# Two-block transformer kernel on one core: expert weight slots that give each partition two neighbouring rows

## The chip, the cores and the metric

The kernel runs on one core of a Trainium2 chip. The metric is the device time of one execution in microseconds (us), lower is better; a run's time is the median over several executions. Every time below is in us unless it is marked ns.

## The reference, cut to what matters

The program computes two transformer blocks on 512 rows of 1024 floats, all in float32. The first block has two layers. Each layer has a mixer (two attentions, a short convolution and gates) and then an expert layer in which each of 16 experts chooses its rows:

```
logits = einsum('bnd,de->ben', h, w_router); aff = softmax(logits, axis=1)
gate, idx = top_k(aff, cap)            # cap = 2 n / 16: 64 rows of x, 32 of the context
xs = h[idx]                            # gather: 16 experts x cap rows x 1024
a = einsum('becd,edf->becf', xs, w_g)  # w_g, w_u, w_d: 16 x 1024 x 1024 each, per layer
u = einsum('becd,edf->becf', xs, w_u)
y = einsum('becf,efd->becd', silu(a) * u, w_d)
out = zeros.at[idx].add(y * gate)
```

Layer 0 does this for x (64 rows per expert) and for the context (32 rows per expert) with the same weights; layer 1 for x alone. The expert weights are 3 x 16 x 4 MB = 201 MB in each layer, and every byte of them is read once per layer. The second block has two more attentions and a dense feed-forward layer; it has no experts.

## The kernel before, in words

Five engines run five programs written out by hand. They meet by semaphores, and nothing reorders them: the order on an engine is the order of its program. SyncE (SP) issues nearly all the transfers. TensorE (PE) does the products, the gathers (a product with a matrix of zeros and ones) and the turns (transposes by a product with the identity).

**Where the expert weights go.** An expert weight is cut into pieces of 256 rows x 1024 columns, 1 MB each. A piece goes by one transfer into one slot: 128 partitions x 2048 floats, read as `p (k n)` with k = 2. `expert_loads(l)` makes the list of the 192 pieces of a layer: for each expert four pieces of the gate and four of the up matrix by turns (`inner`, 8 pieces), and after each even expert from the third on the 8 pieces of the down matrices of a pair (`down`). Before the change, partition p of a slot holds rows p and p + 128 of the piece, each a run of 4096 bytes in memory. `sp_experts` (L2640 issues) walks this list: for each piece it waits until the former piece of that slot has been multiplied, and issues the transfer. Layer 1 has 12 slots for its first 12 pieces and 7 that go round after that.

**Who reads them.** `pe_inner` multiplies the gathered rows of expert x with the 8 pieces of its gate and up matrices: for each piece it waits for the arrival, then for k in (0, 1) it takes the 128 contraction rows `kk = 2 * k2 + k`. L1925 and L1928 are these products in layer 0 and L1920 in layer 1. `pe_outer` does the same with the down matrices of a pair (L1959 and L1964 in layer 0, L1955 in layer 1), and frees two slots at a time. `pe_back` (L1850, L1854) puts the results back into the rows of x.

**Who decides which rows of the contraction a tile holds.** The gathers write the gathered rows with the contraction (the 1024 features) over the partitions: tile k takes 128 feature columns of the normalised rows `H2h`, `H2l` (high and low part) as the stationary operand, and the choice matrix `SX` or `SC` as the moving one. L1546 is the gather of the context (layer 0, 32 matmuls), L1572 in `pe_gather` is the gather of x (128 matmuls in layer 0; 64 in layer 1 ahead of the experts, and 192 more, in 24 steps of 8, between the products of experts 1 to 9: `late_steps`, `pe_late`). The turns of `pe_flip` (L1900) do the same for the hidden rows ahead of the down product: tile j takes 128 columns of `hw`, as the stationary operand, against the identity (6 turns per expert in layer 0, 4 in layer 1).

Two operations elsewhere in the program are of use for comparison. L2276, in the second block, turns tiles of `XT` whose stationary operand takes every fourth column, 16 bytes apart. The table `k_rope` is loaded once, 1 MB with 2048 floats (8192 bytes) in one run per partition.

Names used below: e0 and e1 are the expert stages of layers 0 and 1. A row `ps<-sx,h2h` is a matmul whose moving operand is `sx` and whose stationary one is `h2h`; its LDWEIGHTS row (PEld) loads the stationary one.

Of the kernel before, what the change touches and what calls it, by code (L numbers as in the profile page):

```python
# [236 lines left out]
def build(nc, I, cst, cmask, crope, at, out):  # L237
    ctx = ExitStack()
    with ctx:
# [43 lines left out]
        def signals(*names):  # L283
            made = [Signal(sem(n)) for n in names]
            SIG.extend(made)
            return made
# [9 lines left out]
            "d_wg", "d_xo", "r_dve", "e_hb", "e_ht", "e_st", "d_lz", "d_ff", "d_an", "d_out")  # L296
        l_rc, l_na, l_ma, l_h2, l_an = signals("l_rc", "l_na", "l_ma", "l_h2", "l_an")

        class Mem:
            pass  # L300

# [38 lines left out]
        for l in (0, 1):  # L340
# [3 lines left out]
            n = (2, 4)[l]  # L344
# [11 lines left out]
        ident = K("ident")  # L356
# [31 lines left out]
        SX, SXf = (sx[:, :].bitcast(t).rearrange("p (t e c) -> p t e c", t=4, e=16) for t in (F32R, F32))  # L388
        SC, SCf = (sc[:, :].bitcast(t).rearrange("p (t g r e c) -> p t g r e c", t=2, g=8, r=2, e=2) for t in (F32R, F32))
# [63 lines left out]
        def expert_loads(l):  # L453
            found = []

            def add(name, src, *freed):
                srcs = [(lambda b: b.rearrange("p (k n) -> p k n", k=2), src.rearrange("(k p) n -> p k n", p=128))]
                found.append((name, ES[l].add(srcs, SLOT, "plain", freed)))

            def inner(e):  # L460
                for k2 in range(4):
                    for w, name in enumerate(("w_e_gate", "w_e_up")):
                        add(("in", e, k2, w), I[name][l][e][256 * k2:256 * k2 + 256, :], e_in, f"e{l}", e, k2, w)

            def down(p):
                for f2 in range(4):
                    for x in (0, 1):
                        add(("dn", p, f2, x), I["w_e_down"][l][2 * p + x][256 * f2:256 * f2 + 256, :], e_dn, f"e{l}", p, f2)

            for e in range(NE):  # L470
                inner(e)
                if e % 2 == 0 and e:
                    down(e // 2 - 1)
            down(NE // 2 - 1)
            return found
# [998 lines left out]
        def pe_choice(e, l):  # L1474
# [7 lines left out]
            ps, when = bank.take((st, "lgp"), r_act.at(st, "lgp"))  # L1482
# [4 lines left out]
            for k in range(KD):  # L1487
                e.wait_ge(*r_act.at(st, "h", k))
                for a, b in segs(T):
                    i = e.matmul(ps[32 * (k % 4):32 * (k % 4) + 32, a:b], wr[:, 128 * l + 16 * k:128 * l + 16 * k + 32], HT[:, k, a:b],  # L1490
                                 start=k < 4, stop=k > 3, skip_group_check=True)
            i.then_inc(*p_rt.up(st, "lgp"))
            mods(*range(80, 88))
            ps, when = bank.take((st, "lg"), r_dve.at(st, "af"))
# [3 lines left out]
            for c in range(ntc):  # L1498
                i = e.matmul(ps[:, 16 * c:16 * c + 16], L_[1][:, 128 * c:128 * c + 128], K("fold"), start=c == 0, stop=True, skip_group_check=True)
# [3 lines left out]
            ps, when = bank.take((st, "E"), r_dve.at(st, "E"))  # L1503
# [3 lines left out]
            for c in range(ntc):  # L1507
                i = e.transpose(ps[0:16, 128 * c:128 * c + 128], affT[:, c, :], ident)
            i.then_inc(*p_rt.up(st, "E"))
            for c in range(ntc):  # L1510
                ps, when = bank.take((st, "h2", c), r_act.at(st, "h2", c))
                for w in when:
                    e.wait_ge(*w)
                for k in range(KD):
                    i = e.transpose(ps[:, k * 128:(k + 1) * 128], HT[:, k, c * 128:(c + 1) * 128], ident)
# [4 lines left out]
            ps, when = bank.take((st, "mk"), r_dve.at(st, "m"))  # L1520
# [3 lines left out]
            for c in range(ntc):  # L1524
                i = e.transpose(ps[:, 16 * c:16 * c + 16], L_[3][0:16, c * 128:(c + 1) * 128], K("ident")[0:16, 0:16])
            i.then_inc(*p_rt.up(st, "mk"))
            ps, when = bank.take((st, "cum"), r_dve.at(st, "pos"))
# [4 lines left out]
            for a, b, cap, c0, c1 in sides:  # L1532
                for j in range(c0, c1 - 1):
                    i = e.matmul(ps[:, 16 * j + 16:16 * c1], ones[:, :], mskT[:, j:j + 1, :].broadcast_to([128, c1 - 1 - j, 16]), start=False,
                                 stop=j == c1 - 2, skip_group_check=True)
            i.then_inc(*p_rt.up(st, "cum"))
            if l == 0:
                e.wait_ge(*r_dve.at(st, "sc", 1))
                e.wait_ge(*l_h2.at(st, ntc - 1))
                for k in range(KD):  # L1540
                    ps, when = bank.take((st, "xc", k), r_act.at(st, "xc", k))
                    for w in when:
                        e.wait_ge(*w)
                    for c in (0, 1):
                        for p, h2 in enumerate((m.H2h, m.H2l)):
                            i = e.matmul(ps[:, 0:512], h2[:, 4 + c, k * 128:(k + 1) * 128], SC[:, c, :, 0].rearrange("p g e c -> p g (e c)"),  # L1546
                                         start=c == 0 and p == 0, stop=c == 1 and p == 1)
                    i.then_inc(*p_rt.up(st, "xc", k))
            e.wait_ge(*l_h2.at(st, ntc - 1))
# [4 lines left out]
            for tiles in jobs:  # L1554
                taken = []
                for k, part in tiles:
                    ps, when = bank.take((st, "xs", k, part), gathered(l, k, part))
                    taken.append(ps)
                    for w in when:
                        e.wait_ge(*w)  # L1560
                for c in (1, 2, 3, 0):
                    e.wait_ge(*r_dve.at(st, "sx", c))
                    for ps, (k, part) in zip(taken, tiles):
                        pe_gather(e, l, ps, k, part, c)

        def gathered(l, k, part):
            return (r_dve if (k % 2 if l else part) else r_act).at(f"e{l}", "xs", k, part)

        def pe_gather(e, l, ps, k, part, c):
            m, n = ME[l], 4 if l else 8  # L1570
            for p, h2 in enumerate((m.H2h, m.H2l)):
                i = e.matmul(ps[:, 0:64 * n], h2[:, c, k * 128:(k + 1) * 128], SX[:, c, n * part:n * part + n, :].rearrange("p e c -> p (e c)"),  # L1572
                             start=c == 1 and p == 0, stop=c == 0 and p == 1)
            if c == 0:
                i.then_inc(*p_rt.up(f"e{l}", "xs", k, part))
# [7 lines left out]
        def pe_late(e, k, part):  # L1583

            e.wait_ge(*c_lz.at("e1", last_round(1) - 1))
            if k:
                e.wait_ge(*r_act.at("e1", "xs", k - 1, part))
            elif part > 1:
                e.wait_ge(*r_act.at("e1", "xs", KD - 1, part - 1))
            for c in (1, 2, 3, 0):  # L1590
                pe_gather(e, 1, late_tile, k, part, c)
# [134 lines left out]
        P0, P1, PC, P3 = bank.tiles  # L1726
# [158 lines left out]
        def pe_flip(e, l, x):  # L1885
            st = f"e{l}"
            if x == 0:
                e.wait_ge(*c_lz.at(st, last_round(l) - 1))
            if x:
                e.wait_ge(*e_ht.at(st, x - 1))  # L1890
            if l == 0:
                if x:
                    e.wait_ge(*e_si.at(st, x - 1, "hc"))
                p = (x - 1) // 2 - 1
                if p >= 1 and p % 2 and x % 2:
                    e.wait_ge(*d_xo.at(st, p, KD - 1))
            e.wait_ge(*e_hb.at(st, x))
            hw = HW1[x % 3] if l else HW0[x % 2]
            for j in range(4 if l else 6):
                i = e.transpose(P3[:, 128 * j:128 * j + 128], hw[:, 128 * j:128 * j + 128], ident)  # L1900
            i.then_inc(*e_tr.up(st, x))

        def pe_inner(e, l, x):
# [64 lines left out]
        def pe_experts(e, l):  # L1968
            st = f"e{l}"
            for tile, freed in bank.queue:  # L1970
                for w in freed:
                    e.wait_ge(*w)
            for x in range(NE):
                pe_inner(e, l, x)
                if l and x:
                    pe_flip(e, l, x - 1)
                p = x // 2 - 1
                if x % 2 == 0 and x:
                    pe_outer(e, l, p)
                if x % 2 and p >= 0 and batch(l, p):  # L1980
                    pe_back(e, l, p)
            pe_flip(e, l, NE - 1)
            pe_outer(e, l, MANY - 1)
            pe_back(e, l, MANY - 1)
            read = (d_xo.at(st, MANY - 1, KD - 1),)
            normed = (n_ln.at(f"n{l + 1}"),)
            bank.start((normed, read, read, read) if l else (read, read, normed, read))
# [589 lines left out]
        def pe_program(e):  # L2577
            pe_start(e)
            for l in (0, 1):
                pe_proj(e, l)  # L2580
                projected(e, l)
                pe_attention(e, AT[l])
                attended(e, l)
                pe_merge(e, l)
                pe_choice(e, l)
                pe_experts(e, l)
            pe_second(e)
# [143 lines left out]
```

## Time and profile before

| | |
|---|---|
| time, median of 3 runs | 3599.14 us (3598.61 to 3600.02) |
| span of the profiled execution | 3596.7 us |
| PE busy | 3375.6 us, 94% of the span |
| PE weight loads (PEld) | 2272.8 us, 63% |
| DVE, ACT, POOL busy | 35%, 28%, 5% |
| moved by DMA | 601.35 MB, of which 403 MB are expert pieces (384 of 1 MB) |

The span goes from the first to the last instruction of one execution. No other time of that execution is given; the timed runs are 2.4 us longer at their median, which is what lies around the span. A busy share is an average over stages with different limits; the busy time of PE also counts matmuls whose ends are modelled.

### The profile page before, as it was taken

Reading aid. Unit: us, or ns where it says so; the run is one execution under the profiler, and the core shown is the slowest. Engines: PE = TensorE matmul, PEld = TensorE weight load, DVE = VectorE, ACT = ScalarE, POOL = GpSimd, SP = SyncE. Lnnn points to the kernel's source line nnn. Section 1 sums busy time; section 2 is a strip of 40 time slices with the busy share of each in tenths; the row PEclk is TensorE's granted clock in tenths of the full one; section 3 lists DMA queues with packets and bytes.
Section 4 is the critical chain, followed back from the end, with each engine's and each line's share of the span. In section 5 each row is a group of like instructions: output and inputs, shape, how many; then the busy total and the mean of one; then the engine's idle time right before and its main releaser. Section 6 shows DMA issues by size and latency. Waiting matters only on the chain.

```text
span 3596.7 us, 48683 instructions
## 1 busy us (share of the span) xinstructions
PE 3375.6 (94%) x21614; PEld 2272.8 (63%) x21618; DVE 1241.8 (35%) x1745; ACT 1023.8 (28%) x1641; POOL 197.5 (5%) x118
## 2 busy tenths in 40 slices
PE   7999999999899999989999998898879999989998
PEld 5787667887544443467768874333227766868887
DVE  3235642223421111144563343111124434353333
ACT  3523541213310000036353232000012344243323
POOL 0100000211100000001000221000001010020000
PEclk9999999999899999999999998999999999999999
DMA  7440014222499889822102327999992121323332
GB/s 227 132 139 24 1 51 123 61 65 88 172 372 400 345 340 398 333 65 81 37 1 77 94 82 290 409 408 409 409 336 76 37 57 30 97 62 94 99 98 67
DMA packets 360129, 601.35 MB, mean 167 GB/s; under 512 B 48786, under 2 KB 242672, under 8 KB 359792
## 3 DMA queue, kind: packets, MB, share of 16 engines
q1 hardware_dynamic: 357024, 596.62, 46.8%
q8 instruction: 171, 2.80, 0.3%
q10 hardware_dynamic: 2896, 1.61, 0.2%
q14 instruction: 38, 0.31, 0.0%
HBM read 596.09 MB, written 2.10 MB: 166 GB/s over the span
## 4 chain that ended last, share of the span: by engine, by line
PE 85%; DMA 7%; DVE 5%; ACT 2%; issue 1%; ACTq 0%; POOL 0%; DVEq 0%; SPq 0%
PE ps L581 32%; PE ps L1925 6%; PE ps L2303 5%; PE ps L1075 4%; PE ps L1920 4%; PE ps L633 3%; PE ps L1164 3%; PE ps L1928 3%; PE ps L1959 3%; PE ps L1125 3%; PE ps L1339 3%; DMA ring<-in_w_e_down 3%; DMA ring<-in_w_e_up 2%; PE ps L602 2%; PE ps L1955 2%; PE ps L1850 2%
## 5 line engine op out<-in xcount | busy, mean ns | idle before, releaser
L581 PE MATMUL ps<-xh,wh 128*128 128x512 f32 x1912 | 647.2, 377 | 20.0 <-DVE xl L2142 9.8
L581 PE MATMUL ps<-xh,wl 128*128 128x512 f32 x1912 | 631.6, 368 | 0.0
L581 PE MATMUL ps<-xl,wh 128*128 128x512 f32 x1912 | 630.1, 368 | 0.0
L554 DVE TENSOR_TENSOR wl<-ring,wh 128x1024 fp32r<-128x1024 f32 (+1 forms) x259 | 333.9, 1289 | 441.0 <-ACT wh L545 439.4
L581 PEld LDWEIGHTS ps<-xh,wh 128*128 128x128 f32 x1912 | 330.4, 189 | 105.9 <-issue 33.3
L545 ACT ACTIVATE wh<-ring 128x1024 fp32r<-128x1024 f32 (+1 forms) x259 | 271.9, 1050 | 424.1 <-PE ps L581 163.2
L581 PEld LDWEIGHTS ps<-xl,wh 128*128 128x128 f32 x1912 | 329.8, 189 | 63.5 <-issue 4.5
L581 PEld LDWEIGHTS ps<-xh,wl 128*128 128x128 f32 x1912 | 329.5, 189 | 61.4
L1925 PE MATMUL ps<-ring,arena 128*32 128x512 f32 x2048 | 267.3, 594 | 1.0 <-DVE arena L1707 1.0
L1920 PE MATMUL ps<-ring,arena 128*64 128x512 f32 x984 | 227.0, 599 | 17.4 <-DMA ring<-in_w_e_up 8.7
L1920 PEld LDWEIGHTS ps<-ring,arena 128*64 128x64 f32 x984 | 66.6, 137 | 155.3 <-issue 102.7
L1928 PEld LDWEIGHTS ps<-ring,arena 128*32 128x32 f32 x2048 | 66.8, 110 | 152.9 <-issue 152.9
L1086 DVE TENSOR_REDUCE sm<-ps 128x2 f32<-128x1536 f32 (+3 forms) x96 | 142.3, 1482 | 50.4 <-PE ps L1075 50.2
L1928 PE MATMUL ps<-ring,arena 128*32 128x256 f32 x2048 | 157.5, 379 | 0.0
L1075 PE MATMUL ps<-arena 64*128 64x256 f32 (+3 forms) x800 | 152.1, 455 | 2.6 <-DVE arena L1035 1.8
L1125 PE MATMUL ps<-consts,tmp 128*128 128x128 f32 x832 | 127.1, 285 | 20.3 <-DVE arena L1181 12.0
L1104 ACT ACTIVATE tmp<-ps,sm 128x768 f32<-128x768 f32 (+3 forms) x176 | 132.5, 761 | 46.2 <-DVE sm L1089 38.8
L1955 PE MATMUL ps<-ring,arena 128*64 128x512 f32 x512 | 119.3, 618 | 26.6 <-DMA ring<-in_w_e_down 18.9
L2080 DVE SCALAR_TENSOR_TENSOR y<-ps,gate,y 128x1024 fp32r<-128x1024 f32 x16 | 20.5, 1284 | 306.8 <-ACT y L2015 306.8
L1125 PEld LDWEIGHTS ps<-consts,tmp 128*128 128x128 f32 x832 | 88.5, 141 | 58.9 <-issue 21.9
L1959 PE MATMUL ps<-ring,hbuf 128*32 128x512 f32 x1024 | 121.8, 592 | 0.8 <-DVE hbuf L2072 0.8
L1463 POOL TENSOR_TENSOR arena<-arena,tmp 128x768 f32<-128x768 f32 (+1 forms) x32 | 65.8, 2058 | 991.3 <-DVE tmp L1421 991.3
(278 smaller groups left out, 4329.8 us busy)
## 6 DMA issues: line engine op xcount, KB each, us to landing
ring<-in_w_e_gate SPq DMA_DIRECT2D x128, 1024.0 KB, 9.4
ring<-in_w_e_down SPq DMA_DIRECT2D x128, 1024.0 KB, 8.7
ring<-in_w_e_up SPq DMA_DIRECT2D x123, 1024.0 KB, 9.3
ring<-in_w_in SPq DMA_DIRECT2D x116, 512.0 KB, 3.9
ring<-in_w_ada SPq DMA_DIRECT2D x96, 512.0 KB, 4.7
ring<-in_w_ff SPq DMA_DIRECT2D x64, 512.0 KB, 3.9
ring<-in_w_out SPq DMA_DIRECT2D x24, 512.0 KB, 3.6
ring<-in_w_in SPq DMA_DIRECT2D x40, 256.0 KB, 3.9
```

The lines of the kernel that those rows point to most:

```text
L545: e.activation(m.WH[:, o:o + many], halves.aps[s][:, 0:many], ACT.Copy).then_inc(*hi.up(X.key, q))
L554: e.tensor_tensor(m.WL[:, o:o + many], halves.aps[s][:, 0:many], m.WH[:, o:o + many].bitcast(F32), ALU.subtract).then_inc(*lo.up(X.key, q))
L581: i = e.matmul(ps[0:M, a:b], w[:, k, 0:M], h[:, k, a:b], start=k == 0 and p == 0, stop=k == 7 and p == 2)
L1075: x = e.matmul(ps[:, col:col + k.shape[-1]], q, k, start=first, stop=last, skip_group_check=True)
L1086: e.tensor_reduce(mx, A.units(i, A.scores(i)), AX, ALU.max).then_inc(*a_rm.up(A.stage, i))
L1125: x = e.transpose(ps[:, 128 * c:128 * c + 128], src[:, u, 128 * b:128 * b + 128], ident)
L1920: i = e.matmul(pa[64 * h:64 * h + 64, 512 * w:512 * w + 512], rows_of(1, kk, x, 0, 64), W[:, k, 512 * h:512 * h + 512], start=kk == 0, sto ...
L1925: e.matmul(pa[64 * h + g:64 * h + g + 32, 512 * w:512 * w + 512], rows_of(0, kk, x, g, g + 32), W[:, k, 512 * h:512 * h + 512], start=kk = ...
L1928: i = e.matmul(pb[32 * q:32 * q + 32, 256 * w:256 * w + 256], rows_of(0, kk, x, 64, 96), W[:, k, 256 * q:256 * q + 256], start=kk == 0 and ...
L1955: i = e.matmul(ps[64 * x:64 * x + 64, 512 * h:512 * h + 512], HT2[p % 2][:, x, k % 4, k // 4, :], w, start=k == 0, stop=k == 7)
L1959: e.matmul(ps[64 * x + g:64 * x + g + 32, 512 * h:512 * h + 512], HX[:, k, 64 * x + g:64 * x + g + 32], w, start=k == 0, stop=k == 7, skip ...
L2303: i = e.matmul(ps[:, n:n + 512], ff_part(h, f)[c], w[:, 0, n:n + 512], start=f == 0 and p == 0, stop=f == 31 and p == 2, skip_group_check= ...
```

## The change

It touches four lines and adds a helper. The transfer of an expert piece now gives partition p rows 2p and 2p + 1 of the piece, which lie side by side in memory: one run of 8192 bytes instead of two of 4096. The slot is as large as before, its address and the number of transfers too. The products still read the slot by k = 0 and 1, so that k now stands for the even and the odd rows of the piece. To match, the tile that is multiplied with k must hold every second feature: `woven(k)` takes, out of the 256 columns of a piece, every second one, beginning at k % 2. It stands in the gathers of the context and of x and in the turns, each time as the stationary operand, whose columns are then 8 bytes apart instead of 4. Instructions, their order, their waits and their sizes are the same on PE, DVE, ACT and POOL; on SP the 384 transfers of expert pieces read 128x2048 instead of 128x2x1024.

```diff
@@ in build
+        def woven(k, o=0):
+
+            a = o + 256 * (k // 2) + k % 2
+            return slice(a, a + 255, 2)
@@ in expert_loads
             def add(name, src, *freed):
-                srcs = [(lambda b: b.rearrange("p (k n) -> p k n", k=2), src.rearrange("(k p) n -> p k n", p=128))]
+                srcs = [(lambda b: b, src.rearrange("(p k) n -> p (k n)", k=2))]
@@ in pe_choice (the context's gather, L1546)
-                            i = e.matmul(ps[:, 0:512], h2[:, 4 + c, k * 128:(k + 1) * 128], SC[:, c, :, 0].rearrange("p g e c -> p g (e c)"),
+                            i = e.matmul(ps[:, 0:512], h2[:, 4 + c, woven(k)], SC[:, c, :, 0].rearrange("p g e c -> p g (e c)"),
@@ in pe_gather (L1572)
-                i = e.matmul(ps[:, 0:64 * n], h2[:, c, k * 128:(k + 1) * 128], SX[:, c, n * part:n * part + n, :].rearrange("p e c -> p (e c)"),
+                i = e.matmul(ps[:, 0:64 * n], h2[:, c, woven(k)], SX[:, c, n * part:n * part + n, :].rearrange("p e c -> p (e c)"),
@@ in pe_flip (L1900)
-                i = e.transpose(P3[:, 128 * j:128 * j + 128], hw[:, 128 * j:128 * j + 128], ident)
+                i = e.transpose(P3[:, 128 * j:128 * j + 128], hw[:, woven(j)], ident)
```

## Rows read from the trace of the kernel before

**Rows 1.** The page: moved by DMA in 40 slices of 90 us.

```profile
PE   7999999999899999989999998898879999989998
DMA  7440014222499889822102327999992121323332
GB/s 227 132 139 24 1 51 123 61 65 88 172 372 400 345 340 398 333 65 81 37 1 77 94 82 290 409 408 409 409 336 76 37 57 30 97 62 94 99 98 67
```

**Rows 2.** Windows: e0, start of e1, rest of e1, behind it.

```profile
core 0: us, PE busy (x) PEld busy (x) DVE busy (x) ACT busy (x) POOL busy (x), PEclk, DMA share, GB/s
988.00:1545.00 557.00, 552.92 (x5968) 227.84 (x5968) 89.20 (x146) 47.31 (x104) 0.00 (x0) 1.00 0.93 359
2193.00:2240.00 47.00, 46.96 (x237) 19.39 (x238) 9.07 (x11) 9.07 (x23) 0.00 (x0) 1.00 0.82 304
2240.00:2672.00 432.00, 378.16 (x1682) 141.13 (x1684) 66.83 (x92) 23.49 (x41) 0.00 (x0) 0.98 1.02 407
```

**Rows 3.** Waits of PE in e0 (three rows), then in e1 (three rows).

```profile
PE ps L1900 <- DVE tmp L2059: 1.9, 1, 1.9
PE ps L1925 <- DVE arena L1707: 1.0, 1, 1.0
PE ps L1959 <- DVE hbuf L2072: 0.8, 1, 0.8
...
PE ps L1955 <- DMA ring<-in_w_e_down: 18.9, 13, 2.0
...
PE ps L1920 <- DMA ring<-in_w_e_up: 8.7, 15, 0.9
PE ps L1920 <- DMA ring<-in_w_e_gate: 7.9, 16, 0.6
```

**Rows 4.** The chain that ended last, in one pair of e1: start, us, what.

```profile
2559.84 9.85 DMA ring<-in_w_e_down
2569.82 3.65 PE ps L1955 x16
2573.48 1.73 PE ps L1920 x8
2575.23 14.91 DMA ring<-in_w_e_up
2590.18 1.96 PE ps L1920 x8
```

**Rows 5.** DMA queue in 2240:2672: packets, MB, share of 16 engines.

```profile
DMA packets 45528, 175.67 MB, mean 407 GB/s; under 512 B 2687, under 2 KB 2687, under 8 KB 45511
...
q1 hardware_dynamic: 45511, 175.42, 101.9%
```

**Rows 6.** The same in 3300:3320, where only runs of 512 bytes are loaded.

```profile
DMA packets 4013, 2.04 MB, mean 102 GB/s; under 512 B 64, under 2 KB 4012, under 8 KB 4012
...
q1 hardware_dynamic: 4012, 2.02, 34.5%
```

**Rows 7.** The same in 2691.5:2693.4, inside a 1 MB load of k_rope, 8192-byte runs.

```profile
DMA packets 94, 0.77 MB, mean 405 GB/s; under 512 B 0, under 2 KB 0, under 8 KB 0
...
q1 hardware_dynamic: 94, 0.77, 97.0%
```

**Rows 8.** SP's issues at the end of a round of e1: start, took.

```profile
2345.10 0.37 SPq L2640 DMA_DIRECT2D ring<-in_w_e_gate  x1
2356.28 0.37 SPq L2640 DMA_DIRECT2D ring<-in_w_e_up  x1
```

**Rows 9.** Weight loads, ns min/median/max: gather, turn, turn with columns 16 bytes apart.

```profile
L1572 PEld LDWEIGHTS ps<-sx,h2h x192: 186/188/331, 956.9 to 2464.1; 128*128 128x128 f32 x192
L1900 PEld LDWEIGHTS ps<-consts,tmp x160: 137/141/145, 1026.2 to 2660.8; 128*128 128x128 f32 x160
L2276 PEld LDWEIGHTS ps<-consts,arena x32: 195/208/231, 3206.0 to 3222.9; 128*128 128x128 f32 x32
```

**Rows 10.** PE's timeline: six turns of L1900, eight turns of L2276.

```profile
1026.19 0.87 PE L1900 MATMUL ps<-consts,tmp 128*128 128x128 f32 x6
...
3222.08 1.23 PE L2276 MATMUL ps<-consts,arena 128*128 128x128 f32 x8 [0.88 <-ACT tmp L740]
```

**Rows 11.** The chain: both gathers of layer 0, then gathers of e1.

```profile
946.26 9.79 PE ps L1546 x32
956.92 30.23 PE ps L1572 x128
...
2183.01 9.32 PE ps L1572 x64
...
2213.41 1.15 PE ps L1572 x8
```

## The prediction

> **What bounds the kernel now.** I began with the page's slices, because the change touches the transfers of the expert weights and these lie in two places only. The reader is to see two plateaus in the GB/s line: slices 11 to 16 (counted from 0) at 333 to 400, with dips, and slices 25 to 28 at 408 or 409 without any [rows 1]. A flat top at one value looks like a limit of the transfers, a plateau with dips like a queue that waits for someone.
>
> The windows by stage say which. In e0 (557 us) PE is busy for 552.9 us and the DMA moves 359 GB/s. In the main part of e1 (2240 to 2672, 432 us) PE is busy for only 378 us and the DMA share is 1.02 at 407 GB/s [rows 2]. The waits of PE confirm it. In e0 the three rows shown are all it has as waits of its matmuls, 3.7 us together, and none is for a transfer; in e1 the matmuls wait 35.5 us for the three kinds of expert pieces [rows 3]. The chain of work that ended last agrees: in one pair of e1 it runs through transfers for 9.85 and 14.91 us out of some 61 [rows 4]. Where it runs through PE instead, PE is working on pieces while the transfers behind it go on at the full rate, so the pace of these 432 us is the transfers' own. The first 47 us of e1 are still PE's (46.96 busy, 304 GB/s) [rows 2]: it works off the 12 pieces that were loaded ahead.
>
> So: e0 is bound by PE, e1 from 2240 on by the DMA engines, the rest of the program has no expert pieces in it.
>
> **The transfers, part 1: what one piece costs now.** In 2240:2672 queue 1 moved 175.42 MB, which is 167 pieces of 1.049 MB [rows 5]. That is 432 / 167 = 2.58 us a piece; without the short stretch at the end, where the last piece is waited for, it is 1.049 MB / 409 GB/s = 2.56 us [rows 1]. Each of the 16 engines carries 1/16 of a piece: 16 packets of 4096 bytes before, 8 of 8192 after. What counts is whether a packet has a cost that does not grow with its bytes. From the rows: 101.9% of 16 engines x 432 us is 7043 us; of the 45,511 packets 2,687 are under 512 bytes (completion writes, a few ns each, about 25 us together), which leaves 7018 us / 42,824 = 163.9 ns for 4096 bytes [rows 5]. In a window with runs of 512 bytes only, 34.5% x 16 x 20 us = 110.4 us for 3,948 packets, 27.9 ns each [rows 6]. A straight line through both has 136.0 ns / 3584 bytes = 0.0379 ns a byte, and 8.5 ns that do not depend on the bytes. By it a packet of 8192 bytes takes 319 ns. One load of the trace has such packets, the table k_rope with 8192 bytes a partition: 97.0% x 16 x 1.9 us = 29.5 us for 94 packets, 314 ns each [rows 7]. So runs of 8192 bytes do travel as one packet (none of the 94 is under 8 KB), and cost less than twice 163.9.
>
> **Part 2: the gain per piece.** By the line it is 8 x 8.5 = 68 ns of each engine's time, by the k_rope row 16 x 163.9 - 8 x 314 = 110 ns. The second window is 1.9 us of one load, whose edges cut packets; the first comes from two windows of 432 and 20 us. I take 75 ns, near the first: 2.56 us becomes 2.49, or 422 GB/s. 167 pieces x 75 ns = 12.5 us, with 11.4 and 18.4 us as the ends. PE does not become the bound by it: its waits for pieces, 35.5 us, are longer than the gain [rows 3].
>
> The Trainium skill has a rule on this cost (DMA: Bandwidth & Descriptors, "Why small descriptors are slow"): on trn2 a packet pays some 3 cycles beside its 32-byte beats. At the 850 MHz of the same page's specifications that is 3.5 ns, 8 x 3.5 = 28 ns a piece, and an estimate of 4.7 us for the 167. The rows show 8.5 ns where this rule has 3.5; the measured one is used, and the smaller gain stands among the rivals.
>
> **Part 3: where less than that arrives.** Layer 1 has 7 slots that go round. At the end of a round PE frees none while it puts results back, and gathers: SP issues at 2345.10 and then at 2356.28, 11.2 us apart [rows 8]. The queue must last that long. Five pieces in it at 2.56 us are 12.8 us, at 2.49 they are 12.4: the margin shrinks by 0.4 us and is still positive, but the new transfer needs some tenths to start. Seven rounds at 0 to 0.4 us; I take 0.5 us in all, at most 2.6.
>
> In e0 nothing is gained: PE never waits for a piece there [rows 3]. Its cover is that 359 GB/s are asked for where 407 are to be had; the faster transfers only lengthen SP's own waits for free slots. The load issues keep their number and place, so SP's time and the queue's order do not move.
>
> **Part 4: columns 8 bytes apart in the stationary operand.** No row shows a step of 8 bytes. The bounds are the contiguous load (nothing added) and the turns of L2276, whose stationary operand is every fourth float, 16 bytes apart: their load takes 208 ns at the median where that of L1900, the same size and contiguous, takes 141, +67 ns [rows 9]. But most of it is hidden: eight such turns take 1.23 us, 154 ns each, six contiguous ones 0.87, 145 each, so the price that shows is 9 ns a turn [rows 10]. A step of 8 bytes lies between the two. Counts on the path: e0 has 96 turns, 32 and 128 gather matmuls, all on PE, which bounds that stage. At 9 ns these 256 make 2.3 us. Ahead of e1 there are 64 gather matmuls, 0.6 us. In the gathers of layer 0 a matmul takes 30.23 us / 128 = 236 ns against a load of 188 [rows 9, 11], so there is room for 48 ns; in those of e1, with half the columns, 9.32 us / 64 = 146 ns [rows 11], the load is already longer than the step, and a longer one may show in full: 64 x 67 ns = 4.3 us. The 192 late gathers and the 64 turns inside e1 stand beside the waits for transfers; their cover is the 35.5 us of those waits, and without it they would cost 9 to 67 ns each, 2.3 to 17 us. I take 1.0 us for all of it, and 0 and 7 us as the ends.
>
> The Trainium skill has a rule here too (SBUF — State Buffer, the note on "cachelines"): an SBUF line is 16 bytes, and two hits in a line are enough for full bandwidth. At 16 bytes apart there is one hit, and the trace's 208 ns against 141 agrees. At 8 bytes there are two, which by that rule costs nothing; the sum would then be 1 us better.
>
> **The sum.** -12.5 + 0.5 + 1.0 = -11.0 us. The profiled execution has a span of 3596.7, so 3585.7 is expected of the changed one; the timed runs lie 2.4 us above it, which makes 3588 against the median of 3599.1. This is 0.31% faster. A measurement of this kernel can tell about 0.2% (7.2 us) from no change.
>
> **The rivals.**
>
> *A. Half of the fixed cost was hidden already.* The share of 101.9% says that packets overlap: 16 x 163.9 = 2622 ns of packet time fit into 2564 ns, so 58 of the 136 ns of fixed time (16 x 8.5) are covered by a neighbour. If only the exposed 78 ns are halved, a piece gains 39 ns and the stage 6.5 us: 3594 with the costs above. Against it: fewer, longer packets have no reason to lose their overlap. The Trainium skill's three cycles a packet, above, would end near here, at 3596 by the same costs.
>
> *B. The bytes are the limit.* If the 16 engines or the memory deliver 409 GB/s whatever the run, nothing is gained: 3600 with the costs. For it: the flat 408 to 409 over four slices, and 405 GB/s in the k_rope window. Against it: that window has a share of only 97%, which scales to 417, while the plateau needs 102%.
>
> *C. The ring runs dry, PE takes over.* A new transfer that comes a microsecond late in each of seven rounds takes back 7 us: 3595. For it: the issues 11.2 us apart. Against: one slice at most dips, to 408.
>
> *D. Slower: the gathers wait for their weight loads.* If a step of 8 bytes doubles the load to 376 ns and none of that is hidden, layer 0 pays 160 x (376 - 236) = 22 us and layer 1 ahead of its experts 64 x (376 - 146) = 15 us, which makes 3599.1 - 12 + 37 = 3624. It decides from 12 us / 224 matmuls = 54 ns shown per gather matmul. Against it: four floats apart shows 9 ns, and two cannot well be worse.
>
> **How the numbers follow.** The forecast has 0.72, A 0.10, B 0.07, C 0.04, D 0.07. The forecast's own range is 3582 to 3591 (ends of parts 2 and 4, without both at their worst at once). To leave out no more than 2 in 10, the range takes in A and C and not B and D: 3582 to 3596. Faster by over 0.2% (below 3591.9): the forecast and a little of A, 0.74. Within 0.2%: the rest of A, B and C, 0.19. Slower: D, 0.07.
>
> **What would show it.** The GB/s plateau of slices 25 to 28 at 420 to 424, packets of 8192 bytes at 310 to 320 ns by share and count; e1 from its first product to its last 12 us shorter, e0 within 2 us of 557; PE's waits for pieces down from 35.5 to about 24 us; LDWEIGHTS of L1572's successor within 188 to 210 ns, its 128 matmuls in 30 to 32 us. Wrong would be a plateau still at 409 (B), waits of PE in e0 for loads, or the gathers of layer 0 at over 37 us (D).

## The result and the profile after

The changed kernel takes 3590.43 us at the median of 9 runs, before 3599.63 us (9 runs); the ratio of the two is 0.9975 with a 95% interval of 0.9966 to 0.9983, so 9 us (6 to 12) are gained. One of the 9 runs took 5697.81 us at a mean granted clock of 0.555, where the others have 0.98; the ratio leaves it out, and why so little was granted is not known. The profiled execution has a span of 3589.6 us, 7.1 less than that of before; it took 3591.38 us, 1 us above the median. Run again twice, on two chips, the changed kernel gave ratios of 0.9978 (0.9968 to 0.9988) and 0.9979 (0.9970 to 0.9988).

From the page of the changed kernel, the rows that answer to [rows 1], and the packets:

```profile
PEclk9999999999899999999999998999999999999999
DMA  7440014222499889822102326999982121323331
GB/s 228 133 138 24 1 49 124 63 65 84 175 370 401 340 338 398 346 65 71 48 1 71 96 87 259 420 420 420 421 326 77 38 60 28 99 59 96 98 99 66
DMA packets 310977, 601.35 MB, mean 168 GB/s; under 512 B 48786, under 2 KB 242672, under 8 KB 261488
```

The plateau of e1 stands at 420 or 421 where it was 408 or 409. The program has 49,152 packets fewer than before (310,977 where there were 360,129), and 49,489 that are not under 8 KB where there were 337: the 384 pieces travel as 128 packets each. The hills of e0 (slices 11 to 16) have hardly changed.

The DMA queue in a stretch of 400 us in the middle of e1, as in [rows 5]:

```profile
DMA packets 23072, 168.10 MB, mean 420 GB/s; under 512 B 2565, under 2 KB 2565, under 8 KB 2565
...
q1 hardware_dynamic: 23058, 167.89, 101.1%
```

101.1% x 16 x 400 us = 6470 us; less 23 us for the 2,565 completion writes, which is the estimate of some 9 ns each that the prediction made, 6447 us are left over 20,493 packets, or 314.6 ns for 8192 bytes. One piece takes 1.049 MB / 420 GB/s = 2.497 us where it took 2.564: 67 ns less.

The two expert stages, before the change and after it (columns as in [rows 2]). Each goes from the start of its first expert product to the end of its last; in e0 the last eight products of the context, which end 0.8 or 0.9 us later in every kernel, are left out. Before:

```profile
988.10:1542.90 554.80, 552.08 (x5964) 227.84 (x5968) 89.04 (x145) 46.11 (x102) 0.00 (x0) 1.00 0.94 361
2193.00:2676.50 483.50, 429.48 (x1936) 161.78 (x1936) 75.90 (x103) 32.56 (x64) 0.00 (x0) 0.98 1.00 394
```

After:

```profile
1523.90:1527.30 3.40, 3.40 (x20) 1.08 (x16) 0.00 (x0) 0.00 (x0) 0.00 (x0) 0.50 0.39 161
987.08:1545.27 558.19, 555.50 (x5964) 230.38 (x5968) 88.98 (x145) 46.11 (x102) 0.00 (x0) 1.00 0.91 358
2195.80:2667.70 471.90, 423.53 (x1936) 160.37 (x1936) 75.47 (x103) 32.56 (x64) 0.00 (x0) 1.00 0.98 402
```

e1 is 11.6 us shorter, e0 3.4 us longer. The first row is inside e0: for 3.4 us, at the start of the last down product, the granted clock is 0.50, its lower level of 1.2 GHz; in the profile of before it is at full speed there. A half clock over 3.4 us of PE's work costs 1.7 us. The remaining 1.1 us between -8.2 and -7.1 go in small steps: 1.0 us less was used ahead of e0, 0.4 us more between e0 and e1 (0.56 in the gathers ahead of e1, a little less elsewhere), and 1.7 us more behind e1, where the half clock lasts for 20.5 us, in two stretches from 2670.8 and 2687.8 on, instead of 13.7 in one.

The weight loads of the gathers and turns (ns min/median/max), and six turns on PE's timeline, the rows of after to [rows 9] and [rows 10]:

```profile
L1577 PEld LDWEIGHTS ps<-sx,h2h x192: 193/195/330, 956.4 to 2460.0; 128*128 128x128 f32 x192
L1905 PEld LDWEIGHTS ps<-consts,tmp x160: 194/209/219, 1025.1 to 2652.4; 128*128 128x128 f32 x160
```

```profile
1025.13 0.98 PE L1905 MATMUL ps<-consts,tmp 128*128 128x128 f32 x6
```

The turn's load takes 209 ns with columns 8 bytes apart, as much as L2276's with 16 (208), and 141 when contiguous. Six turns last 0.98 us instead of 0.87: 18 ns each. (Single matmuls of the trace show that half of it falls on the first step of a group, 221 ns instead of 164, and 11 ns on each of the four that follow.) The gather's load grows by only 7 ns. From the chain, the gathers themselves, to [rows 11]:

```profile
945.57 9.96 PE ps L1551 x32
956.40 29.70 PE ps L1577 x128
...
2185.20 9.88 PE ps L1577 x64
```

In layer 0 they are as long as before (9.8 and 30.2 us), ahead of e1 0.56 us longer. But most of the 0.56 us is the clock's. Here are the windows of these 64 matmuls in four kernels: before, changed, and two from the experiments below, layer 0 alone (contiguous columns here) and layer 1 alone, second profile (every second column here).

```profile
2183.00:2192.30 9.30, 9.29 (x64) 9.11 (x64) 4.55 (x6) 1.53 (x4) 0.00 (x0) 0.82 1.03 410
2185.20:2195.10 9.90, 9.87 (x64) 9.67 (x64) 4.53 (x6) 1.54 (x4) 0.00 (x0) 0.78 1.01 422
2185.90:2195.70 9.80, 9.78 (x64) 9.60 (x64) 4.56 (x6) 1.54 (x4) 0.00 (x0) 0.78 1.03 411
2182.90:2192.30 9.40, 9.40 (x64) 9.21 (x64) 4.49 (x6) 1.53 (x4) 0.00 (x0) 0.82 1.02 424
```

A granted clock of 0.82 means that the gathers began with 3.4 us of half clock, one of 0.78 that they began with 4.3. With 3.4 us the chain gives 9.32 us contiguous (before) and 9.47 woven (layer 1 alone); with 4.3 us it gives 9.80 contiguous (layer 0 alone) and 9.88 woven (changed). The weave costs 0.1 us of it, 1 to 2 ns a matmul, and the clock 0.4 to 0.5. Last, PE's waits for pieces in e1, to [rows 3]:

```profile
PE ps L1960 <- DMA ring<-in_w_e_down: 15.2, 12, 2.7
...
PE ps L1925 <- DMA ring<-in_w_e_up: 6.8, 13, 0.6
PE ps L1925 <- DMA ring<-in_w_e_gate: 5.8, 13, 0.6
```

27.8 us instead of 35.5: PE still waits for the transfers, and e1 is still theirs. The waits fell by 7.7 us where e1 fell by 11.6, and PE's own work in e1 fell too, from 429.5 to 423.5 us; its granted clock there was 0.98 before and is 1.00 now. That clock does not set the length of e1: the turns' kernel below has 1.00 there and the transfers of before, and its e1 lasts 483.5 us.

### The profile page after: what moved, and what is told of

Read it like the earlier page. It is cut to its first block, busy times and chain, and to the rows that moved or that the text cites. A ratio compares the mean times of both kernels' runs of the same rounds, so it can differ in the third digit from the quotient of the medians.

```text
span 3589.6 us, 48687 instructions
## 1 busy us (share of the span) xinstructions
PE 3376.1 (94%) x21618; PEld 2276.8 (63%) x21618; DVE 1241.2 (35%) x1745; ACT 1023.8 (29%) x1641; POOL 197.6 (6%) x118
## 2 busy tenths in 40 slices
DMA packets 310977, 601.35 MB, mean 168 GB/s; under 512 B 48786, under 2 KB 242672, under 8 KB 261488
## 4 chain that ended last, share of the span: by engine, by line
PE 86%; DMA 5%; DVE 5%; ACT 2%; issue 1%; ACTq 0%; POOL 0%; DVEq 0%; SPq 0%
PE ps L586 32%; PE ps L1930 6%; PE ps L2308 5%; PE ps L1080 4%; PE ps L1925 4%; PE ps L638 3%; PE ps L1169 3%; PE ps L1964 3%; PE ps L1933 3%; PE ps L1130 3%; PE ps L1344 3%; DMA ring<-in_w_e_up 2%; PE ps L1960 2%; PE ps L607 2%; PE ps L1577 2%; DMA ring<-in_w_e_down 2%
## 5 line engine op out<-in xcount | busy, mean ns | idle before, releaser
L1960 PE MATMUL ps<-ring,arena 128*64 128x512 f32 x512 | 114.1, 595 | 25.1 <-DMA ring<-in_w_e_down 15.2
L2085 DVE SCALAR_TENSOR_TENSOR y<-ps,gate,y 128x1024 fp32r<-128x1024 f32 x16 | 20.5, 1284 | 302.3 <-ACT y L2020 302.3
```

Source lines behind the costliest of these rows:

```text
L1960: i = e.matmul(ps[64 * x:64 * x + 64, 512 * h:512 * h + 512], HT2[p % 2][:, x, k % 4, k // 4, :], w, start=k == 0, stop=k == 7)
```

## The experiments

Two parts stand in the change, the runs and the weave. Four kernels take them apart by part and by layer, two more take the weave apart, and one doubles the packets instead of halving them. The time of before is always that of the same chip. The edits are cut to the expressions that differ. Lengths of e0 and e1 are those of the profiled execution, measured as above.

**Runs alone.** The changed kernel with contiguous columns; the contraction then pairs the wrong rows. Edit:

```diff
-h2[:, 4 + c, woven(k)]   h2[:, c, woven(k)]   hw[:, woven(j)]
+h2[:, 4 + c, k * 128:(k + 1) * 128]   h2[:, c, k * 128:(k + 1) * 128]   hw[:, 128 * j:128 * j + 128]
```

> This kernel has the runs of 8192 bytes alone: gathers and turns take contiguous columns as before, so the contraction pairs the wrong rows and the output is not the reference's. My theory (packets have a fixed cost of some 9 ns; the weave costs on PE) says: e1 shorter by 12 us as in the changed kernel, e0 as long as before, so about 3587, 2 to 3.5 us below the changed kernel. Rival (the weave costs nothing, the 3.4 us lost in e0 are chance of the clock): equal to the changed kernel within 1 us, and the turns' weight loads at 141 ns all the same.

Measured: 3588.2 us against 3598.74, ratio 0.9968 (0.9956 to 0.9979). e0 and e1:

```profile
988.50:1543.30 554.80, 552.07 (x5964) 227.39 (x5968) 89.02 (x145) 46.11 (x102) 0.00 (x0) 1.00 0.91 360
2193.50:2665.30 471.80, 423.53 (x1936) 159.21 (x1936) 75.87 (x103) 32.56 (x64) 0.00 (x0) 0.99 0.98 403
```

e0 is as long as before, e1 11.7 us shorter. The turns' loads are back at 140 ns. So the whole gain is the runs', it lies in e1, and the 3.4 us of e0 come with the weave. The changed kernel took 3591.41 us beside it, 3.2 us more.

**Weave alone.** The changed kernel with the transfers of before (the contraction pairs the wrong rows):

```diff
-srcs = [(lambda b: b, src.rearrange("(p k) n -> p (k n)", k=2))]
+srcs = [(lambda b: b.rearrange("p (k n) -> p k n", k=2), src.rearrange("(k p) n -> p k n", p=128))]
```

> This kernel has the weave alone: stationary operands of gathers and turns take every second column, the transfers give two runs of 4096 bytes as before, so the output is not the reference's. My theory: e1 as long as before (483.5 us from its first product to its last, because its weave hides behind the transfers), e0 longer by 1.6 us for 96 turns, perhaps 1.7 more where the clock falls once; in all 3600 to 3603, 1 to 3 us above before. Rival (all of it is chance): 3599.6, e0 unchanged.

Measured: 3603.38 us against 3598.74, ratio 1.0013 (1.0004 to 1.0021). e0 and e1:

```profile
985.90:1545.30 559.40, 556.69 (x5964) 229.57 (x5968) 89.04 (x145) 46.12 (x102) 0.00 (x0) 0.99 0.93 358
2196.90:2679.70 482.80, 427.43 (x1936) 162.36 (x1936) 75.58 (x103) 32.56 (x64) 0.00 (x0) 0.99 1.00 393
```

e1 is within 0.7 us of before, e0 4.6 us longer. Here the half clock lasts 6.8 us, from 1521.5 on: from the end of the last turns into the last down product. The weave alone makes the kernel slower by 4.6 us at the median, where 1 to 3 had been expected, and by more than its turns take on PE.

**Both parts in layer 1 alone.** The output is the reference's.

```diff
-srcs = [(lambda b: b, src.rearrange("(p k) n -> p (k n)", k=2))]
+srcs = [(lambda b: b, src.rearrange("(p k) n -> p (k n)", k=2)) if l else
+        (lambda b: b.rearrange("p (k n) -> p k n", k=2), src.rearrange("(k p) n -> p k n", p=128))]
-h2[:, c, woven(k)]
+h2[:, c, woven(k) if l else slice(k * 128, (k + 1) * 128)]
-hw[:, woven(j)]
+hw[:, woven(j) if l else slice(128 * j, 128 * j + 128)]
```

The context's gather, which layer 0 alone has, takes contiguous columns again.

> Both parts of the change in layer 1 alone; layer 0 as before. The output is the reference's. My theory: layer 0 is bound by PE, so it gains nothing from longer runs and pays for the weave; without both there the kernel is 1.6 to 3.5 us faster than the changed one, 3587 to 3589, e0 at 554.7 us and e1 at 471.9. Rival (longer runs help layer 0 too, or the weave is free): as fast as the changed kernel or slower, about 3590.4.

> The version with both parts in layer 1 alone once more, beside the changed kernel on the same chip, since the intervals of the first comparison overlap. My theory: e0 as long as before, e1 11.7 us shorter; 3586 to 3589, 2 to 4 us below the changed kernel. Rival (the difference was chance of the clock): the two medians within 1 us.

Measured: 3587.84 us against 3598.74, ratio 0.9965 (0.9953 to 0.9978), and the second time 3588.43 against 3599.59, ratio 0.9967 (0.9955 to 0.9980). The second profile:

```profile
987.90:1542.60 554.70, 552.00 (x5964) 227.32 (x5968) 88.99 (x145) 46.11 (x102) 0.00 (x0) 1.00 0.94 361
2193.00:2664.70 471.70, 423.19 (x1936) 160.25 (x1936) 75.56 (x103) 32.55 (x64) 0.00 (x0) 1.00 0.98 403
```

e0 as before, e1 11.8 us shorter. In the first profile e1 is 472.0 us and e0 556.4, 1.7 us over before, with the half clock for 3.4 us from 1520.4 on, although layer 0 is not woven there. So that fall needs no weave.

**The changed kernel again, twice.**

> The changed kernel once more beside the others, for a second profile. If the clock's fall at 1524 us of the first profile belongs to the changed kernel (its turns last 0.1 us longer there), it stands in this profile too; if it is chance of that execution, it is absent and e0 is 1.6 to 1.7 us longer than before instead of 3.4. Time 3590.4 within 1.5 us.

> The changed kernel a third time, as the other side of that comparison: 3589 to 3592; its e0 3.3 to 3.5 us longer than before if the clock falls again at the start of the last down product, 1.7 if not.

Measured: 3591.41 against 3598.74, and 3592.89 against 3599.59. e0 lasts 558.0 and 557.9 us, e1 472.2 and 471.4, and the half clock stands at 1523.0 and 1524.0 for 3.4 us both times. The second median is 0.9 us above what was expected. Against the version of layer 1 on the same chip these medians are 3.6 and 4.5 us higher. The intervals of the ratios overlap, but the runs hardly do: all five of that version lie below all eight of the changed kernel the first time, and below ten of its eleven the second. That version is the better one, by more than the turns alone.

**Twice the packets.** The kernel before with runs of 2048 bytes (the slot then holds other rows and halves of rows than the products assume):

```diff
-srcs = [(lambda b: b.rearrange("p (k n) -> p k n", k=2), src.rearrange("(k p) n -> p k n", p=128))]
+srcs = [(lambda b: b.rearrange("p (c n) -> p c n", c=4),
+         src.rearrange("r (h n) -> (r h) n", h=2).rearrange("(c p) n -> p c n", p=128))]
```

> The kernel before with runs of 2048 bytes: each partition of a slot gets four of them, from places 256 KB apart, so the contraction pairs the wrong rows and the output is not the reference's. Same bytes, same number of transfers, twice the packets (32 instead of 16 per engine and piece). My theory (8.7 ns per packet that do not depend on its bytes): a piece takes 2.56 + 16 x 0.0087 = 2.70 us, a plateau of 388 GB/s in e1, e1 longer by 167 x 0.139 = 23 us or a little more; e0 longer by 0 to 5 us where its bursts need the full rate; 3622 to 3628. Rival A (half of the fixed cost hidden by overlap): +12 us. Rival (long runs only matter from 4096 bytes on, or what was gained is the memory's access to neighbouring rows): the plateau stays at 409, 3599, or it moves by another amount than 139 ns.

Measured: 3624.12 us (4 runs) against 3597.94, ratio 1.0067 (1.0053 to 1.0080). The page's slices, the queue in 2300:2650, and the windows of e0 and e1:

```profile
GB/s 227 134 135 23 1 59 117 59 65 121 171 369 375 359 351 386 329 42 87 24 1 94 94 72 346 386 387 387 387 331 87 39 48 38 97 64 93 97 97 69
```

```profile
DMA packets 68043, 135.30 MB, mean 387 GB/s; under 512 B 2060, under 2 KB 2060, under 8 KB 68031
...
q1 hardware_dynamic: 68031, 135.12, 104.6%
```

```profile
985.80:1540.60 554.80, 552.09 (x5964) 227.71 (x5968) 89.00 (x145) 46.11 (x102) 0.00 (x0) 1.00 1.00 360
2190.70:2699.30 508.60, 429.10 (x1936) 159.83 (x1936) 75.87 (x103) 32.56 (x64) 0.00 (x0) 0.99 1.03 376
```

The plateau is 387 (388 was expected), so a piece takes 2.710 us. With 32, 16 and 8 packets per engine a piece takes 2.710, 2.564 and 2.497 us: 9.1 ns for each of the first 16 packets saved, 8.4 ns for each of the next 8. The rates are whole GB/s, so these two can be off by up to 0.8 ns and are the same within that. e1 is 25.1 us longer, 167 x 0.146 = 24.4 us of it by this count. e0 does not change, even with slower transfers: it has room to spare. The bytes alone are not the limit (rival B): they are the same at 387, 409 and 420 GB/s. The rival of the memory's neighbouring rows is not needed: the runs of a partition lie apart before and in this kernel, and the step between these two is the same per packet as the step to the changed kernel, where they lie side by side. No run has short packets from neighbouring places alone.

**Gathers alone, turns alone.** The kernel before with `woven` in the two gathers only, and in the turns only (in both the contraction pairs the wrong rows):

```diff
-h2[:, 4 + c, k * 128:(k + 1) * 128]   h2[:, c, k * 128:(k + 1) * 128]
+h2[:, 4 + c, woven(k)]   h2[:, c, woven(k)]
```

```diff
-hw[:, 128 * j:128 * j + 128]
+hw[:, woven(j)]
```

> The kernel before with the weave in the two gathers alone (4096-byte runs, contiguous turns; the output is not the reference's). My theory: layer 0's gathers keep their 30.2 and 9.8 us (a matmul of 512 columns covers the load), the 64 ahead of e1 cost 0.55 us; 3599 to 3600, within 1 us of before. Rival (the gathers carry the cost that the trace does not show in the turns): 3601 to 3603.

> The kernel before with the weave in the turns alone (4096-byte runs, contiguous gathers; the output is not the reference's). My theory: 96 turns of layer 0 at 18 ns each, 1.7 us in e0, nothing in e1; 3600.5 to 3602, 1.7 to 3 us above before. Rival (the cost of the weave lies in the gathers or in the clock): within 0.5 us of before, whatever its weight loads last.

Measured, gathers: 3598.23 against 3597.94, ratio 0.9998 (0.9989 to 1.0007), e0 554.8 us. Turns: 3601.67 against 3597.94, ratio 1.0010 (1.0001 to 1.0019). The windows of the turns' kernel: e0, a piece of it, and e1.

```profile
985.70:1545.10 559.40, 556.67 (x5964) 229.99 (x5968) 89.07 (x145) 46.12 (x102) 0.00 (x0) 0.99 0.93 358
1521.00:1527.80 6.80, 5.97 (x33) 1.83 (x35) 0.69 (x1) 0.38 (x1) 0.00 (x0) 0.50 0.55 219
2196.20:2679.70 483.50, 425.68 (x1936) 160.92 (x1936) 75.43 (x103) 32.55 (x64) 0.00 (x0) 1.00 0.99 393
```

The gathers' weave cannot be told from nothing, the turns' costs 3.7 us at the median, where 1.7 to 3 had been expected. In the profile e0 is 4.6 us longer: 96 turns x 18 ns = 1.7 us, and a half clock of 6.8 us, of which PE was idle for 0.8. Nothing shows in e1.

**Both parts in layer 0 alone**, the counterpart of the version above (the output is the reference's):

```diff
+srcs = [(lambda b: b.rearrange("p (k n) -> p k n", k=2), src.rearrange("(k p) n -> p k n", p=128))] if l else \
+       [(lambda b: b, src.rearrange("(p k) n -> p (k n)", k=2))]
+h2[:, c, slice(k * 128, (k + 1) * 128) if l else woven(k)]
+hw[:, slice(128 * j, 128 * j + 128) if l else woven(j)]
```

> Both parts of the change in layer 0 alone; layer 1 as before. The output is the reference's. My theory: layer 0 has no use for faster transfers and pays for the turns, so e0 is 1.6 to 1.8 us longer than before (3.4 with a fall of the clock) and e1 unchanged; 3600.5 to 3603. Rival (longer runs help layer 0, through its bursts or the memory): below 3598.

Measured: 3602.37 against 3597.94, ratio 1.0009 (1.0000 to 1.0018), only just told from nothing. e0 558.2 us with a half clock of 3.4 us, e1 483.9. In layer 0 the change only costs.

## Why the prediction was right

3588.0 was forecast and 3582 to 3596 given; 3590.4 came, 0.25% below before. The likeliest case is the one that happened, with the gain and the cost both nearer to the bad end than I took them. Of the signs that were named, three missed: e0 grew by 3.4 us and not within 2, PE's waits fell to 27.8 us and not to 24, and the 128 gathers of layer 0 took 29.7 us and not 30 to 32. The 2.4 us that the text above puts around the span are not that: each later run has its own span on record, 1.8 us below its time (3589.6 and 3591.38 here). The other 0.6 us were the distance of one profiled execution from a median.

*What bounds each stage.* Right. e0 gains nothing from faster transfers and loses nothing from slower ones (554.8 us with runs of 2, 4 and 8 KB); e1 takes them one for one.

*Parts 1 and 2, the packets.* Right in kind: a packet has a cost beside its bytes. By the line through 512 and 4096 bytes a piece should gain 68 ns, and 67 came; the 75 ns that I took leaned towards the k_rope row for no good reason, 1.3 us too much. That row was true of something else: 314 ns per packet was forecast by it, and 314.6 was measured. But the packet times fell by 16 x 163.9 - 8 x 314.6 = 106 ns a piece and the period by 67; their share went from 102.3% of a piece's period to 100.8%, so they overlap less. To that extent rival A was right: part of what is saved per packet had been hidden, though more than its 39 ns arrived. That the line gave 68 was luck. Measured in the full queue, packets of 2048, 4096 and 8192 bytes take 88.5, 163.9 and 314.6 ns, which is 0.0368 ns a byte and 13 ns beside it; the line had 8.5 ns, with its lower point from a window where the queue was busy for 34.5%. Too small a cost by the packet times, all of it counted as gain, came out like the right cost of which two thirds arrive. The sum must be made in periods, not in packet times. The Trainium skill's three cycles, or 3.5 ns a packet (DMA: Bandwidth & Descriptors, "Why small descriptors are slow"), are too small for this case: the runs show 8.4 to 9.1 ns.

*Part 3, what arrives of it.* No ring ran dry: e1 shortened by 11.3 to 12.1 us in the three profiles of the changed kernel and the two of the version of layer 1, against 167 x 67 ns = 11.2 us. The 0.5 us reserved for it were not used.

*Part 4, the weave.* The mechanism was right, the size was not: 1.0 us was set for all of it. The term that was mis-sized is the 9 ns a turn; a turn costs 18 ns more in groups of six, 1.7 us in e0. My bound came from eight turns of L2276 and six of L1900 on the timeline. Each average holds a slow first step and the end of the last turn once per group, which eight turns share out thinner than six. The first six of those eight turns, in the trace of before, give the right price:

```profile
3222.08 0.99 PE L2276 MATMUL ps<-consts,arena 128*128 128x128 f32 x6 [0.88 <-ACT tmp L740]
```

0.99 us against 0.87 is 20 ns a turn, close to the 18 that came. I had put the load of a step of 8 bytes between 141 and 208 ns; it takes 209, the whole price of 16 bytes. Here the Trainium skill (SBUF — State Buffer, the note on "cachelines") says that two hits in a 16-byte line keep full bandwidth, and the measurement does not agree for the weight loads of turns: 8 bytes apart costs as much as 16. Of the gathers, those of layer 0 came out right: nothing shows under matmuls of 512 columns. Ahead of e1 0.56 us came where 0.6 was put at 9 ns a matmul, but that is luck: 0.1 us is the weave's, at 1 to 2 ns, and the rest the clock's. Their 146 ns a matmul in the prediction were an average over two levels of the clock too. Rival D, which lived from the gathers, did not happen.

*What I did not have.* The clock. Six profiled kernels have woven turns in layer 0 (the changed one three times, the weave alone, the turns alone, layer 0 alone), and all six show a stretch of half clock that begins between the last turns of e0 and the first 0.3 us of its last down product, and lasts 3.4 or 6.8 us, 1.4 to 3 us of time. Of the six profiles without woven turns there (before, runs alone, 2 KB runs, gathers alone, layer 1 twice) one shows it (layer 1 alone, first profile, from 1520.4 on, with the down product begun at 1520.0). At that place PE waits 1.9 us for the last hidden rows, turns them, and waits 0.8 us again before the product, and the turns are longer now. That the weave makes the fall likelier is what the counts suggest; the one unwoven case shows that it is not needed, and no run was made that shifts the turns without weaving. It stays open. With it, -11.6 (e1) + 1.7 (turns) + 1.7 (clock in e0) + 0.6 (gathers ahead of e1) = -7.6, of which the 0.6 too are mostly the clock's. The rest to the profiled -7.1 is -1.0 ahead of e0, -0.2 between e0 and e1 and +1.7 behind e1. The last of these goes with 6.8 us more of half clock. The 1.0 us ahead of e0 is not the clock's: it is there in full when DVE begins on L688 (L683 before) at 46.57 us instead of 47.64, ahead of the first stretch of half clock (49.3 us), and its cause is open.

## What to carry to other kernels

A transfer-bound stage whose plateau is flat pays per packet as well as per byte: doubling the run from 4 to 8 KB gave 2.7% of its rate, halving it took 5.4%. Make such an edit only in the stage that is bound by transfers, because the layout has a price elsewhere; here layer 1 alone gives 11 us, both layers 7 to 9. Judge it from the period of a transfer (bytes by plateau rate), since packet durations overlap and overstate the gain.

## What the hardware showed unexpectedly

- A weight load of 128 float columns for a turn takes 141 ns contiguous and 208 or 209 ns with columns 8 or 16 bytes apart, but only 18 ns of it show per turn; the load of a gather's operand (type float32r in the kernel) goes from 188 to 195 ns, and 1 to 2 ns of that show ahead of e1.
- A load of packets of 8192 bytes takes 314.6 ns each, of 4096 bytes 163.9, of 2048 bytes 88.5 (104.6% x 16 x 350 us less completion writes, over 65,971): 13 ns of each do not grow with its bytes. The periods of a piece are only 8.4 to 9.1 ns per packet apart.
- The lower level of the clock over 3.4 us, at one place, is 1.7 us of a 3600 us kernel, nearly a fifth of the gain that was to be measured.
